# Two layer norms of a two-block decoder: residual loads, weight buffers and GpSimd passes placed anew

## The reference

```python
for i in range(DEPTH):
    h = ssd_mixer(x, ...) if i % 2 == 0 else dsa_mixer(x, ...)
    x = layer_norm(DN_ALPHA * x + h, ln_g[i], ln_b[i])
...
h = x
for i in range(DEPTH):
    hn = rms_norm_2(h, norm_g[i])
    h = h + (gmlp_branch(hn, ...) if i % 2 == 0 else stick_breaking_branch(hn, ...))
return rms_norm_2(h, final_g)
```

## Time and profile before

| | us |
|---|---|
| median of 3 runs | 2516.5 (2514.34 to 2516.64) |
| the profiled execution | 2514.76 |
| its span on the core | 2513.5 |
| TensorE busy in it | 2448.9 |
| VectorE busy | 1568.8 |
| ScalarE busy | 1242.2 |
| GpSimd busy | 103.9 |

### The profile page before, as it was taken

How to read it: one execution, slowest core, us unless ns; L and a number is a source line. 1 busy time by engine, 2 the same in 40 slices (tenths; PEclk the granted TensorE clock), 3 DMA queues, 4 the chain that set the end, 5 groups by cost and what they waited for, 6 DMA issues and landing times.

```text
span 2513.5 us, 45354 instructions
## 1 busy us (share of the span) xinstructions
PE 2448.9 (97%) x19640; PEld 2352.9 (94%) x19640; DVE 1568.8 (62%) x2065; ACT 1242.2 (49%) x1431; POOL 103.9 (4%) x62
## 2 busy tenths in 40 slices
PE   8999999998989999998989999999999999999998
PEld 7999999998979999998978889999999999999998
DVE  5778888864566766665575456565655455555556
ACT  3445665553455555553354444454444445454453
POOL 0001000100030000000030000000000000000002
PEclk9999999999999999999989999999999999999999
DMA  6765656656636455446546666666655565555644
GB/s 183 226 199 179 212 181 185 184 177 199 221 125 229 153 159 161 150 156 215 195 140 195 188 189 188 193 189 184 189 186 185 193 195 172 178 168 174 186 156 173
DMA packets 263209, 459.53 MB, mean 183 GB/s; under 512 B 18571, under 2 KB 69857, under 8 KB 260577
## 3 DMA queue, kind: packets, MB, share of 16 engines
q1 hardware_dynamic: 263009, 456.63, 58.0%
HBM read 452.18 MB, written 4.26 MB: 182 GB/s over the span
## 4 chain that ended last, share of the span: by engine, by line
PE 92%; DVE 4%; ACT 2%; DMA 1%; issue 1%; SPq 0%; POOL 0%; ACTq 0%; DVEq 0%
PE G L667 86%; PE M L667 5%; PE M L680 1%; DVE XH L1687 1%; DVE AA L1478 1%; DVE W L1474 1%; DMA RES<-in_x 0%; DMA RES<-x_scratch 0%; ACT Z L1183 0%; ACT GH L1183 0%; DMA XS<-in_x 0%; DVE WA L1474 0%; DVE BT L1513 0%; DVE W2m L1474 0%; DVE W0m L1474 0%
## 5 line engine op out<-in xcount | busy, mean ns | idle before, releaser
L667 PE MATMUL G<-AA,W 128*128 128x256 f32 x7884 | 942.7, 278 | 5.9 <-DVE W L1474 5.8
L667 PEld LDWEIGHTS G<-AA,W 128*128 128x128 f32 x7884 | 917.2, 188 | 12.9 <-DVE W L1474 6.8
L1474 DVE TENSOR_TENSOR W<-RAW,W 128x1024 fp32r<-128x1024 f32 x432 | 535.9, 1243 | 372.5 <-ACT W L1074 371.3
L1074 ACT CAST W<-RAW 128x1024 fp32r<-128x1024 f32 x432 | 449.4, 1046 | 445.7 <-PE G L667 430.4
L667 PE MATMUL G<-AA,WY 128*128 128x256 f32 x2532 | 308.1, 278 | 0.0
L667 PEld LDWEIGHTS G<-AA,WY 128*128 128x128 f32 x2532 | 296.0, 188 | 2.5 <-issue 2.2
L1474 DVE TENSOR_TENSOR WY<-RAW,WY 128x1024 fp32r<-128x1024 f32 (+1 forms) x128 | 160.1, 1252 | 99.7 <-ACT WY L1074 99.7
L667 PE MATMUL G<-W,AA 128*128 128x512 f32 x876 | 214.1, 400 | 3.6 <-DVE AA L1478 3.6
L667 PEld LDWEIGHTS G<-W,AA 128*128 128x128 f32 x876 | 165.3, 190 | 44.2 <-DVE AA L1478 4.2
L1074 ACT CAST WY<-RAW 128x1024 fp32r<-128x1024 f32 (+1 forms) x128 | 133.0, 1044 | 142.6 <-PE G L667 138.3
L667 PE MATMUL G<-W0m,YY 128*128 128x256 f32 x1464 | 181.5, 280 | 17.9 <-DVE W0m L1474 17.9
(11 more groups left out here) (289 smaller groups left out, 2428.8 us busy)
## 6 DMA issues: line engine op xcount, KB each, us to landing
RAW<-in_a_w_in SPq DMA_DIRECT2D x192, 512.0 KB, 3.7
RAW<-in_ssd_w_in SPq DMA_DIRECT2D x160, 512.0 KB, 4.4
RAW<-in_b_w_in SPq DMA_DIRECT2D x128, 512.0 KB, 4.2
RAW<-in_dsa_w_in SPq DMA_DIRECT2D x72, 512.0 KB, 3.5
RAW<-in_ssd_w_out SPq DMA_DIRECT2D x64, 512.0 KB, 4.5
RAW<-in_dsa_w_out SPq DMA_DIRECT2D x64, 512.0 KB, 4.0
RAW<-in_a_w_out SPq DMA_DIRECT2D x64, 512.0 KB, 3.6
RAW<-in_b_w_out SPq DMA_DIRECT2D x32, 512.0 KB, 3.9
```

Of the source, the lines that this page charges most:

```text
L667: return e.matmul(o, l, r, start=start, stop=stop, skip_group_check=True)
L1074: e.copy(wh[:, 0:n], RAW[:, v % NR, 0:n]).then_inc(*up(cast_done, "cast", v))
L1474: e.tensor_tensor(wl[:, 0:n], RAW[:, v % NR, 0:n], wh[:, 0:n].bitcast(F), ALU.subtract).then_inc(*up(rest_done, "rest", v))
```

## The change

1. The drain and `ln_open` come earlier: in norm 1 after 22 of the 32 units of o1's first two blocks; in norm 2, whose first two blocks are now interleaved by `pair` as well, after 20 of 32. The residual comes in four DMAs of 512 KB, each with a semaphore of its own that the block of its columns waits for. The first block is added after its last unit, which stands 8 units behind `ln_open` in norm 1 and 10 in norm 2.
2. The spare slots are five in each norm and are dealt out from o1 1's unit 9 and o2 1's unit 7 on.
3. Pieces are taken in the order TURNS; GH has three buffers instead of two; VectorE does the gain of pieces (0,0) and (1,0) out of PSUM, ScalarE of the other six; ScalarE's and VectorE's casts and rests come behind the norm's first steps.
4. GpSimd's passes are cut into pieces of 512 columns and start when the last piece of AA is there. In norm 2 GpSimd does only tokens 0 to 127, and VectorE (`gained`) the other half. ScalarE's squares come later.
5. The small matrices of the MLP are loaded one block earlier.

```diff
@@ Plan
+TURNS = ((0, 0), (0, 1), (0, 2), (1, 0), (1, 1), (1, 2), (0, 3), (1, 3))
...
+        self.pair(("o2", 0), ("o2", 1), 14)
...
-        for i in range(4):
-            extra[f"a{i}"] = (self.blocks["o1", 1][14], first["ms", 0])
-        for i in range(3):
-            extra[f"b{i}"] = (first["o2", 1], first["v5", 1])
+        for i in range(5):
+            extra[f"a{i}"] = (self.blocks["o1", 1][9], first["ms", 0])
+            extra[f"b{i}"] = (self.blocks["o2", 1][7], first["v5", 1])
@@ walk
-        run(("o1", 1), to=14)
-        run(("o1", 0), since=14)
+        run(("o1", 1), to=8)
         drain()
         start("ln_open", 1)
-        start("ln_block", 1, 0)
         tick()
-        run(("o1", 1), ("ln_block", 1, 1), since=14)
+        run(("o1", 1), since=8, to=14)
+        for i in range(2):
+            run(("o1", i), ("ln_block", 1, i), since=14)
...
-        run(("o2", 0))
+        run(("o2", 0), to=14)
+        run(("o2", 1), to=6)
         drain()
...
@@ sync_program, ln_open
-                e.dma_start(RES2[:, :, :], A["x"][0].rearrange("(t p) n -> p t n", p=P)).then_inc(
-                    *landed(d["res1_landed"], "res", 1))
+                to, src = RES2, A["x"][0].rearrange("(t p) n -> p t n", p=P)
...
+            for i in range(4):
+                e.dma_start(to[:, :, 512 * i:512 * i + 512], src[:, :, 512 * i:512 * i + 512]).then_inc(
+                    *landed(res_here[i], "res", s, i))
@@ scalar_program, ln_close
             root(0)
-            yield
-            yield
-            gain(0, 0)
-            yield
+            top(0, 0)
             gain(0, 1)
-            yield
+            top(0, 1)
+            yield
+            gain(0, 2)
             root(1)
...
+                e.wait_ge(*done(("v5", 0)))
                 for t in range(2):
                     for q in range(2):
-                        e.wait_ge(*on("h4", t))
+                        e.wait_ge(*on("x2", t))
@@ vector_program, ln_close
             normal(0, 0)
             normal(0, 1)
-            yield
+            gain(0, 0)
             normal(0, 2)
             normal(0, 3)
...
             if s == 2:
                 for _ in range(6):
                     yield
+                for g in range(4):
+                    gained(1, g)
+                    yield
...
+        def gained(t, g):
+            c = slice(512 * g, 512 * g + 512)
+            e.wait_ge(*on("gains", 2))
+            e.tensor_tensor(RES4[:, t, c], XH[:, t, c], ROWS[:, 0, c], ALU.mult).then_inc(
+                *up(dve_made, "x2_g", t, g))
+            e.wait_ge(*on("x2_g", t, g))
+            e.tensor_tensor(RES4[:, t, c], RES4[:, t, c], ROWS[:, 1, c], ALU.add).then_inc(*up(dve_made, "x2", t))
@@ pool_program, ln_close
-            for t in range(2):
-                to = (XH, RES4)[s - 1][:, t, :]
+            for t in range(3 - s):
                 e.wait_ge(*on("gains", s))
-                e.wait_ge(*on("xt_t2", s, t, 3))
-                e.tensor_tensor(to, XH[:, t, :], ROWS[:, 0, :], ALU.mult).then_inc(*up(pool_made, "gained", s, t))
...
+                e.wait_ge(*on(f"at{s}", 3, 1))
+                for g in range(4):
+                    c = slice(512 * g, 512 * g + 512)
+                    to = (XH, RES4)[s - 1][:, t, c]
+                    e.tensor_tensor(to, XH[:, t, c], ROWS[:, 0, c], ALU.mult).then_inc(
+                        *up(pool_made, "x_g", s, t, g))
+                    e.wait_ge(*on("x_g", s, t, g))
+                    e.tensor_tensor(to, to, ROWS[:, 1, c], ALU.add).then_inc(
+                        *up(pool_made, *(("y1", t) if s == 1 else ("x2", t))))
```

More of the change, by code:

```diff
@@ L261, in program @@
     SQS = place("SQS", [P, 2, 5])
+    GB = place("GB5", [P, 2, 16])
     YY = place("YY", [P, 32, 2, T], R, line=STILL)
@@ L478, in walk @@
         start("ln_open", 2)
-        start("ln_block", 2, 0)
         tick()
-        for i in range(1, 4):
+        run(("o2", 1), since=6, to=14)
+        for i in range(2):
+            run(("o2", i), ("ln_block", 2, i), since=14)
+        for i in range(2, 4):
             run(("o2", i), ("ln_block", 2, i))
@@ L484, in walk @@
         twice(("v5", 0))
-        run(("v5", 1), to=3)
+        run(("v5", 1), to=5)
         start("ev_v5", 0)
-        run(("v5", 1), ("ev_v5", 1), since=3)
+        run(("v5", 1), ("ev_v5", 1), since=5)
         for j in range(2, 8):
+            if j == 7:
+                start("mix_load", 0)
             run(("v5", j), ("ev_v5", j))
         for j in range(8):
+            if j > 0:
+                start("mix_load", j)
             start("mix_w", j)
@@ L534, in sync_program @@
                                     "ki_landed", "ws_landed", "bs_landed", "x1_stored",
-                                    "res1_landed", "res2_landed", "gain1_landed", "gain2_landed",
+                                    "gain1_landed", "gain2_landed",
                                     "fg_landed", "out_stored")}
         fetched = [0]
+        res_here = [signal(f"residual{i}_landed") for i in range(4)]
         x_parts = [signal(f"x{i}_landed") for i in range(5)]
@@ L621, in ln_open @@
                 e.wait_ge(*on("x1s"))
[L622 to L623 removed]
+                to, src = RES4, x1_d[:, :, :].rearrange("t p n -> p t n")
+            for i in range(4):
+                e.dma_start(to[:, :, 512 * i:512 * i + 512], src[:, :, 512 * i:512 * i + 512]).then_inc(
+                    *landed(res_here[i], "res", s, i))
             yield
@@ L655, in finish @@
             yield
-        walk(unit, dict(turn_in=turn_in, dt_task=dt_task, ssd=ssd, ev_ms=ev_ms, mix_w=mix_w, ln_open=ln_open,
+        walk(unit, dict(turn_in=turn_in, dt_task=dt_task, ssd=ssd, ev_ms=ev_ms, mix_load=mix_load, ln_open=ln_open,
                         ln_rows=ln_rows, x1_store=x1_store,
@@ L842, in ln_close @@
             yield
-            for h in range(2):
-                for g in range(4):
-                    b = take("xt2", s, h, g)
-                    e.wait_ge(*on("xn", s, h, g))
-                    for i in range(4):
-                        last = transpose(M[:, b, i * P:(i + 1) * P],
-                                         XH[:, h, (4 * g + i) * P:(4 * g + i + 1) * P], ident[:, :])
-                    last.then_inc(*up(pe_made, "xt_t2", s, h, g))
-                    yield
+            for i, (h, g) in enumerate(TURNS):
+                if i == 3:
+                    yield
+                    yield
+                b = take("xt2", s, h, g)
+                e.wait_ge(*on("xn", s, h, g))
+                for f in range(4 * g, 4 * g + 4):
+                    last = transpose(M[:, b, f % 4 * P:(f % 4 + 1) * P], XH[:, h, f * P:(f + 1) * P], ident[:, :])
+                last.then_inc(*up(pe_made, "xt_t2", s, h, g))
+                yield
             if s == 2:
@@ L1688, in normal, with gain @@
                                 RSD[:, h:h + 1], ALU.subtract, ALU.mult).then_inc(*up(dve_made, "xn", s, h, g))
+            def gain(h, g):
+                n = TURNS.index((h, g))
+                e.wait_ge(*on("xt_t2", s, h, g))
+                if n > 2:
+                    h0, g0 = TURNS[n - 3]
+                    e.wait_ge(*on(f"at{s}", g0, h0))
+                for i in range(4):
+                    f = 4 * g + i
+                    sc, bi = (vc("lg", f), vc("lb", f)) if s == 1 else (GB[:, 0, f:f + 1], GB[:, 1, f:f + 1])
+                    e.tensor_scalar(GH[:, n % 3, i, :], M[:, bank.get(("xt2", s, h, g), 0), i * P:(i + 1) * P],
+                                    sc, bi, ALU.mult, ALU.add).then_inc(*up(dve_made, "gained", s, h, g))
+                here(dve_made, "read", "xt2", s, h, g)
             def tails(h, g):
@@ L1692, in tails @@
                 to = AA[:, 4 * g:4 * g + 4, :, h * P:(h + 1) * P]
-                rest(to[:, :, 1, :], GH[:, (4 * h + g) % 2, :, :], to[:, :, 0, :]).then_inc(
+                rest(to[:, :, 1, :], GH[:, TURNS.index((h, g)) % 3, :, :], to[:, :, 0, :]).then_inc(
                     *up(dve_made, f"at{s}", g, h))
@@ L1709, in ln_close @@
             normal(1, 1)
-            yield
+            tails(0, 2)
+            gain(1, 0)
             normal(1, 2)
             normal(1, 3)
-            tails(0, 2)
+            tails(1, 0)
             yield
-            tails(0, 3)
+            tails(1, 1)
             yield
-            for g in range(4):
-                tails(1, g)
+            for h, g in TURNS[5:]:
+                tails(h, g)
                 yield
```

69 lines of the change are left out of this document (33 added, 36 removed).

## The result

| | before | after |
|---|---|---|
| median of 4 runs, us | 2515.42 (2513.75 to 2516.64) | 2482.13 (2481.47 to 2482.3) |
| span of the profiled execution, us | 2513.5 | 2481.0 |
| TensorE without work in it, us | 64.6 | 40.8 |

The ratio is 0.9868, with a 95% interval of 0.9851 to 0.9885. The kernel is 33.3 us faster. The forecast was 2473.5, so the time lies inside the stated range of 2465 to 2484 but 8.6 us above the forecast. The sign was right; 10 of the 43.1 us did not come, and where they stayed is the question of what follows.

The account below looks back on a forecast made before the run. TensorE was taken as the bound, busy 2448.9 of 2513.5 us, so only idle and low-clock time could be won. Residuals 11.0 + 10.4, norms 11.2 + 9.4 and WS 1.1 sum to 43.1: 2473.5 us, range 2465 to 2484.

Parts of the forecast that it names:

- Residuals: At the two residual additions: earlier issue wins the waits and the low clock behind them, 11.0 and 10.4 us.
- The wait of 9.18 goes: First residual: issued some 22 us earlier, it lands in time, so TensorE's 9.18 us wait disappears.
- 8.5 to 12.3: Weight load issued behind the residual: lands 8.5 to 12.3 us after its issue if only after all of it.
- Norm 1: First norm: of 14.1 us lost, 1.4 stays at a late piece and 1.5 at late rests; 11.2 won.
- H: Norm timetable's zero: when TensorE has done the last block's t = 0 half, 695.7 in norm 1 before.
- Norm 2: Second norm: of 15.1 us lost, 1.4 stays in the head and 4.3 in the tail; 9.4 won.
- the low clock of 0.9: Norm 2's tail: half the price of one low-clock stretch as at the residuals, 0.9 us, added to the waits.
- WS: First WS transpose: its 1.12 us wait for its load goes with loading a block earlier; 1.1 won.
- Weight loads starve: Rival, behind the residuals: each still exposes 5 us with its low stretch, 10 to 14 more, 2486; chance 0.06.
- The passes cost their upper bound: Rival, GpSimd's passes: norm 1 loses 4, norm 2 6.6, with longer low clock; 8.4 more, 2482; chance 0.13.
- The ScalarE rival: Norms wait for ScalarE, not GpSimd; the new order keeps half their loss, 14.6 of 29.2: 2480 to 2486; chance 0.08.
- the slower one: Rival, v5, u5, z5: rotated slots put first rests behind evacuations; from 1.8 us per block gain is eaten; chance 0.02.

Follow-up runs that it names:

- e7: Kernel before with only the early four-piece residual and o2's pairing, four and three spare buffers opened at unit 14: 2492.28 us against 2515.86, ratio 0.9909.
- e9: Changed kernel with four spare weight buffers in each set instead of five: 2487.99 us, ratio 0.989.
- e2: Changed kernel with VectorE's addition of block 0 three steps earlier in VectorE's own list, ahead of the spare units' rests: 2469.96 us, ratio 0.9818.
- e10: e2 with four spare weight buffers in each set instead of five: 2482.73 us, ratio 0.9869.
- e5: e2 with the last two of VectorE's four gain passes of norm 2 put behind three weight rests: 2469.86 us, ratio 0.9818.
- e3: Changed kernel with some weight rests and VectorE's own gain passes made by scalar-tensor-tensor instead of plain tensor-tensor: 2481.94 us, ratio 0.9866.
- e4: Changed kernel with GpSimd's passes 2048 columns wide again and started beside the norm, not behind it: 2495.52 us, ratio 0.9918.
- e8: Changed kernel with GpSimd's passes still behind the norm but 2048 columns wide instead of four of 512: 2489.58 us, ratio 0.9897.
- e6: Changed kernel with only two of four residual pieces loaded at the opening, the other two behind block 1's last unit: 2471.09 us, ratio 0.9827.

## Why the prediction was right, and where it was not

- **Residuals: 21.4 forecast, 9.2 came.** This is the step that failed: "The wait of 9.18 goes", with 0 to 1.0 lost to what is moved past; 5.2 and 7.1 us were lost. Residual 1 keeps 3.41 us of wait and 4.63 - 2.88 = 1.75 of low clock, so 5.9 of 11.0 were won; residual 2 keeps 4.36 + 2.7, so 3.3 of 10.4. The prices themselves were right (e7: 23.6 for both). So was what it said of the weight load behind the residual: it was issued from 578.83 and its cast began at 588.64, 9.8 us later, within the 8.5 to 12.3, and TensorE never waited for it. By the rule of the Trainium skill that the prediction cites (page "DMA: Bandwidth & Descriptors", section "Queues, rings and completion order") the load would signal after the residual; the wait of 6.54 us agrees, though queues that are merely full would give such a wait too. What the working left out is who else stands in line: it followed one load to one unit of TensorE, and took the five buffers that open at the same unit as free. They put five more rests ahead of the addition, and the addition frees the PSUM half that TensorE wants two units after block 0's end. The bytes could have warned: 2.1 MB of residual, 2.6 of spare units and the 4.2 of eight running ones are 8.9 MB, which take the 22 us of lead whole even at some 400 GB/s, and cast and rest of the last come on top. From 576.5 to 598.5 us the core moved 287 GB/s, 6.3 MB. How much of the 21.4 stays away also scatters, as the waits under e9 show; the 9.2 is for the profiled execution.
- **Norm 1: left 1.4 + 1.5, measured 1.14 + 0.59 + 0.70.** H was 690.3; the last piece was there 25.6 us behind it, forecast 26. A rest beside GpSimd took 2.04, forecast 2.05. VectorE's gain of a piece (four instructions) took 1.37 us instead of 1.0, which moved nothing. Won 11.7 instead of 11.2.
- **Norm 2: left 1.4 + 4.3, measured 1.14 + 2.18 + 1.47.** The two waits in the tail were forecast as 2.6 and 0.8; the low clock of 0.9 did not come. Won 10.3 instead of 9.4.
- **WS: 1.1**, won; TensorE waits for no WS load, and the stretch 1450 to 1500 has TensorE busy for all of its 50 us.
- The sum: 5.9 + 3.3 + 11.7 + 10.3 + 1.1 = 32.3, against 32.5 in the spans. The 43.1 of the prediction less the 12.2 of the residuals and plus 1.4 of the norms is the same. That they meet to 0.2 us is in part luck: at the start of the kernel, which the change leaves alone, one wait is 2.01 us instead of 0.34 and one group of 24 matmuls takes 3.04 us instead of 4.62. With the addition moved (e2) the kernel takes 2469.96, and the 21.4 are there.
- **Rivals.** "Weight loads starve" had the place and the size (it said 5 us at each residual, and 2486) but the wrong waiter: TensorE waited for a free PSUM half, not for a weight, and a change in one list mended it. "The passes cost their upper bound" named 2482, the measured time, for a cause that did not occur. The range reached to 2484 for this rival's sake and not for the residuals', so it is luck that it held the measured time. By their mechanism the norms, WS and the price of the residuals were right. The ScalarE rival and the slower one left no trace: behind the last wait of norm 2's tail, at 1298.46, TensorE waits nowhere before 1995 us.
- **Assumed and not priced:** the fifth buffer. The norm's timetable took five for granted; e10 shows 12.8 us on it.

One thing stays open: whether e5 wins anything over e2. Its waits in norm 2 are 0.7 us longer and those on WS 1.2 us longer (1.7 against 0.5), and the low clock behind them is gone; what is left is under what these runs tell apart.

## What to carry to other kernels

When two parts of a change start at the same point of the program, price them together: read each engine's list from that point on, and ask what stands ahead of the one instruction that frees a buffer for TensorE. An instruction that frees PSUM belongs ahead of work whose results are wanted only units later; to let it wait a little in front costs nothing as long as the work behind it has lead. Lead (one more weight buffer) is spent wherever a burst of other work stands in the list, so a new order and its buffers have to be judged together. And passes on GpSimd that read SBUF should be short and lie where VectorE has slack.

## What the runs showed of the hardware

- VectorE's scalar-tensor-tensor and plain tensor-tensor instructions wait for GpSimd alike when both inputs are in SBUF: 1.67 and 2.28 us in both forms, against 0.69 and 1.23 alone (e3). With one input in PSUM the first of them ran unhindered beside the passes (0.41 us for 128x256, after). I had hoped that the form would matter.
- Long and short passes do not cost the same in sum, although each VectorE instruction waits for one pass only: 4.9 to 5.6 us with 2048 columns and 1.7 to 2.4 with 512, for instructions of 0.69 to 1.23 us (e4, e8, after). What counts is how many VectorE instructions TensorE is short of while the passes run.
- TensorE's clock was low behind waits of 3.41 and 4.36 us (granted 0.97 and 0.94 over the 60 us around them; behind the first, 24 matmuls took 4.63 us instead of 2.88) and hardly behind one of 1.57 us (3.04, e6). The granted clock behind the 2.18 and 1.47 us of norm 2 stayed at 1.00 in the kernel after and was 0.98 over the same stretch in e2, whose one wait there was 2.17 us: a short wait may or may not cost it.
